# Differential attention: head squares as one instruction per four heads, sums on VectorE

## The reference, cut to what matters

```python
sc = einsum('bqhcd,bshcd->bhcqs', qb, k) * scale
p = softmax(sc, axis=-1)
a = p[:, :, 0] - lam * p[:, :, 1]
o = einsum('bhqs,bshe->bqhe', a, v)
o = rmsnorm(o, subln_g) * (1.0 - lam_init)   # over the 128 columns of a head
return o.reshape(b, s, nh * 2 * dh) @ w_out
```

## Time and profile before

| what | value |
|---|---|
| median of three launches | 1442.16 us (1442.08 to 1443.78) |
| profiled execution | 1442.12 us, its span 1440.3 us |
| TensorE busy | 1422.6 us, 99% of the span |
| VectorE busy | 858.5 us, 60% |
| ScalarE busy | 747.9 us, 52% |
| granted TensorE clock | 1.00 of full speed |
| differential attention's tasks | about 267 to 307 us of the span |

### The profile page before, as it was taken

One profiled execution on the slowest core, in us unless ns is written; L12 is line 12 of the kernel. 1 busy time (PEld: TensorE's weight loads), 2 busy tenths in 40 slices (PEclk: granted clock), 3 DMA queues, 4 the chain that ended last, 5 costly groups with the idle time before them and its releaser, 6 DMA issues.

```text
span 1440.3 us, 20791 instructions
## 1 busy us (share of the span) xinstructions
PE 1422.6 (99%) x6864; PEld 1184.1 (82%) x6864; DVE 858.5 (60%) x1113; ACT 747.9 (52%) x1216; POOL 90.9 (6%) x115
## 2 busy tenths in 40 slices
PE   9999999999999999999999999999999999999999
PEld 7888888778888888888888988888888898888887
DVE  5555575767555565555655665555657756565654
ACT  6444464656444454444546654444545465465553
POOL 2110110012111000000100000000013000000000
PEclk9999999999999999999999999999999999999999
DMA  9877746315655656556463155566565513555551
GB/s 304 245 224 219 219 155 210 118 59 160 190 189 189 203 162 190 189 187 195 157 219 111 37 160 189 188 187 201 181 208 161 176 60 104 178 167 181 184 183 53
DMA packets 189938, 248.21 MB, mean 172 GB/s; under 512 B 15194, under 2 KB 128101, under 8 KB 189760
## 3 DMA queue, kind: packets, MB, share of 16 engines
q1 hardware_dynamic: 187904, 241.35, 53.1%
q0 software_dynamic: 1984, 6.21, 1.9%
HBM read 246.33 MB, written 1.17 MB: 172 GB/s over the span
## 4 chain that ended last, share of the span: by engine, by line
PE 93%; DVE 3%; ACT 1%; issue 1%; POOL 1%; DMA 0%; SPq 0%; ACTq 0%; DVEq 0%; POOLq 0%
PE ps L272 26%; PE ps L274 26%; PE ps L273 26%; PE ps L760 2%; PE ps L796 2%; PE ps L555 1%; PE ps L785 1%; PE ps L285 1%; DVE h L476 1%; PE ps L367 1%; PE ps L962 1%; PE ps L286 1%; PE ps L290 1%; PE ps L332 1%; PE ps L331 1%
## 5 line engine op out<-in xcount | busy, mean ns | idle before, releaser
L265 DVE TENSOR_TENSOR wlo<-raw,whi 128x1024 fp32r<-128x1024 f32 x450 | 549.5, 1230 | 393.4 <-ACT whi L257 393.2
L257 ACT CAST whi<-raw 128x1024 fp32r<-128x1024 f32 x450 | 469.9, 1051 | 361.5 <-PE ps L274 344.9
L272 PE MATMUL ps<-whi,xhi 128*128 128x512 f32 x1280 | 499.9, 391 | 0.0
L274 PE MATMUL ps<-whi,xlo 128*128 128x512 f32 x1280 | 498.2, 389 | 0.0
L273 PE MATMUL ps<-wlo,xhi 128*128 128x512 f32 x1280 | 498.0, 389 | 0.0
L274 PEld LDWEIGHTS ps<-whi,xlo 128*128 128x128 f32 x1280 | 240.2, 188 | 50.3
L272 PEld LDWEIGHTS ps<-whi,xhi 128*128 128x128 f32 x1280 | 240.3, 188 | 49.5
L273 PEld LDWEIGHTS ps<-wlo,xhi 128*128 128x128 f32 x1280 | 240.3, 188 | 49.3
L272 PE MATMUL ps<-whi,thi 128*128 128x512 f32 x400 | 160.5, 401 | 0.0
L274 PE MATMUL ps<-whi,tlo 128*128 128x512 f32 x400 | 156.4, 391 | 0.0
L273 PE MATMUL ps<-wlo,thi 128*128 128x512 f32 x400 | 156.0, 390 | 0.0
(11 more groups left out here) (181 smaller groups left out, 1141.2 us busy)
## 6 DMA issues: line engine op xcount, KB each, us to landing
raw<-in_ffn_wg_dram SPq DMA_DIRECT2D x176, 256.0 KB, 2.9
raw<-in_ffn_wu_dram SPq DMA_DIRECT2D x176, 256.0 KB, 3.1
raw<-in_ffn_wd_dram SPq DMA_DIRECT2D x176, 256.0 KB, 3.0
raw<-in_w_ffn_up_dram SPq DMA_DIRECT2D x88, 256.0 KB, 3.5
raw<-in_w_in_dram SPq DMA_DIRECT2D x80, 256.0 KB, 3.3
raw<-in_diff_w_in_dram SPq DMA_DIRECT2D x48, 256.0 KB, 3.0
raw<-in_na_w_in_dram SPq DMA_DIRECT2D x48, 256.0 KB, 3.1
raw<-in_w_ffn_down_dram SPq DMA_DIRECT2D x44, 256.0 KB, 3.0
```

The costliest lines, as they stand in the source:

```text
L257: nc.scalar.copy(whi[:, s], raw[:, s]).then_inc(s_hi, 1)
L265: nc.vector.tensor_tensor(wlo[:, s], raw[:, s], whi[:, s].bitcast(F32), ALU.subtract).then_inc(s_lo, 1)
L272: nc.tensor.matmul(outs[t], ahi[:, c], whi[:, s, i], start=start, stop=False)
L274: last = nc.tensor.matmul(outs[t], alo[:, c], whi[:, s, i], start=False, stop=stop)
```

## The change

`squares(g)` becomes one ScalarE instruction over the 512 elements of a PSUM bank, without accumulator, in place of four over 128 elements with one accumulator each. VectorE gets a reduction over four groups of 128 elements, from the buffer of squares `sqa` into `sso`, between the wait for the squares and the product that stood there. Because VectorE now reads the buffer, ScalarE waits before groups 2 and 3 for the sums of two groups earlier (`s_ss`) and no longer for its own squares (`s_sq`).

```diff
@@ -814,12 +814,8 @@
                 act.wait_ge(s_pv, b + 4 * (g + 1))
                 if g >= 2:
-                    act.wait_ge(s_sq, g - 1)
-                for hd in range(4):
-                    ins = nc.scalar.activation(sqa[:, (g % 2) * 512 + hd * P:(g % 2) * 512 + (hd + 1) * P],
-                                               ps[:, Y + g, hd * P:(hd + 1) * P], ACT.Square,
-                                               accum_out=sso[:, g // 2, 4 * (g % 2) + hd:4 * (g % 2) + hd + 1])
-                ins.then_inc(s_sq, 1)
+                    act.wait_ge(s_ss, g - 1)
+                nc.scalar.activation(sqa[:, (g % 2) * 512:(g % 2 + 1) * 512], ps[:, Y + g], ACT.Square).then_inc(s_sq, 1)
@@ -860,6 +856,8 @@
                 steps.done(nc.vector.tensor_tensor(ri[:, t, inv2], ri[:, t, c], ri[:, t, c], ALU.mult))
                 dve.wait_ge(s_sq, g + 1)
+                steps.done(nc.vector.tensor_reduce(sso[:, t, c], sqa[:, (g % 2) * 512:(g % 2 + 1) * 512].rearrange(
+                    "p (g c) -> p g c", g=4), AX_X, ALU.add))
                 nc.vector.tensor_tensor(sso[:, t, c], sso[:, t, c], ri[:, t, inv2], ALU.mult).then_inc(s_ss, 1)
```

## The result

The changed kernel takes 1446.26 us (median of 13 executions, 1444.45 to 1448.01) against 1442.24 us before (median of 13, 1441.89 to 1443.78). The ratio over all executions is 1.0025 with a 95% interval of 1.0016 to 1.0033: slower by about a quarter of a per cent. Between the medians lie 4.0 us. The forecast was 2.4 us and 1444.5, and the measured median lies 0.06 us above the upper end of its range, 1446.2. The executions don't lie around their median but in three clumps: three at 1444.45 to 1444.61, seven at 1445.96 to 1446.36, three at 1447.37 to 1448.01. The first clump is where the forecast put the time; what sets the second apart is the subject of most experiments.

The account below looks back on a forecast made before the run. VectorE was taken to bound the attention's second half and the chain to the last transposes; delays of 0.51 + 0.52 + 0.66 + 0.70 = 2.39 us for groups 0 to 3 gave 1444.5 us, 8-in-10 range 1443.1 to 1446.2.

Parts of the forecast that it names:

- VectorE sets the pace of this stage: Second half of the attention's tasks, 284 to 300 us: VectorE, busy 14.96 of 16 us, is the limit, not TensorE.
- ScalarE's saving is worth nothing: One square per group saves ScalarE about 0.48 us, but VectorE comes later anyway, so nothing is gained on the path.
- the room that the prediction had counted: Slack before VectorE's later instructions in groups 0, 1 and 2, 0.41 us together, already counted as given back.
- The waits cost nothing: ScalarE's new wait for sums of two groups earlier, before groups 2 and 3, finds them ready and costs nothing.
- the delay is carried to the end whole: Behind the last transposes at 306.40 us nothing absorbs the 2.39 us, so the program ends that much later.
- rival 1: TensorE's pause before the last transposes grows to 2.7 us and its clock falls, costing 3.1 us: 1447.6 us, chance 0.07.
- one of the prediction's own signs of being wrong: Matmuls behind the last transposes, after 308.8 us, starting more than 0.23 us apart would show the forecast wrong.
- The price of a fall: A slow TensorE stretch of 6.2 us, as at the program's start, would lose half of it, 3.1 us.
- The other 0.75: Chance of no distinguishable change, below about 0.2% or 2.9 us; it holds most of the forecast and the absorbed delay.
- the dear reduction: VectorE's reduction costs 1.21 us, as for 1024 elements, because of SBUF reading or its groups: 1446.7 us, chance 0.06.
- the absorbed delay: The delay is made up later in the program and the time stays at 1442.2 us; chance 0.06.
- ScalarE's exponentials were the limit: ScalarE's late exponentials limit the tasks and hide the reductions; at most 0.41 us gained, 1441.7 us, chance 0.04.

Follow-up runs that it names:

- e4: Changed kernel with the four accumulating squares kept on ScalarE beside VectorE's reductions: median 1446.10 us, quick group 1444.6.
- e5: Changed kernel without the reductions, one ScalarE square per group, product reading each head's first column: 1441.88 us, ratio 0.9997 to the kernel before.
- e6: Kernel before with 1, 2 or 3 unused VectorE reductions in front of group 3's product: medians 1444.48, 1445.10 and 1445.88 us.
- e1: Changed kernel with eight warming products on TensorE in the pause before the last four transposes: 1444.50 us, ratio 1.0018 to the kernel before.
- e2: Kernel before with the change for head groups 2 and 3 only: median 1445.40 us, quick group 1443.9.
- e3: Kernel before with the change for head groups 0 and 1 only: median 1443.54 us, quick group 1443.5.

## Why the prediction was right and where it was not

- **VectorE sets the pace of this stage:** right. Four reductions, 0.69 us each (0.67 taken), moved the chain by 2.44 us (2.39 forecast), each group within 0.05 us.
- **ScalarE's saving is worth nothing:** right beside the reductions, shown by e4 (same time without it). Without them it is worth 0.4 us (quick groups of e5), as much as the room that the prediction had counted.
- **The waits cost nothing, and the delay is carried to the end whole:** right; behind 313.75 us the matmuls are as dense as before, and the changed kernel's quick executions lie at 1444.5 us, the forecast.
- **The clock:** the step that failed is the chance given to rival 1. The prediction worked out the pause of 2.7 us (2.73 measured), said that the trace had none of this length to test it, and then gave the fall 7 in 100. It came in most executions: 10 of 13 of the changed kernel are late, and the profiled one shows the low clock right behind the pause. e6 shows that lengthening the pause alone does it, e1 that filling it undoes it. With that, one of the prediction's own signs of being wrong came true: matmuls behind the last transposes start 0.43 us apart, not 0.23. The Trainium skill, "TensorE: Matmul & The Clock Gate", section "HAM oscillation — how this bites in real kernels", names idle gaps as the cause. The runs agree on that. The gaps here are shorter than those of its example, and yet 2.05 and 2.7 us were enough in most executions.
- **The price of a fall:** 3.1 us was half of a slow stretch of 6.2 us, taken from the start of the program. Here the granted clock was low only between 309 and 313 us, and that cost 1.59 us in the trace. Between the first two clumps lie 1.5 to 1.7 us in the six kernels with a long pause. A single such fall gives 1446.1 us, not the 1447.6 of the rival.
- **Chances and range:** slower by over 0.2% had 0.23 and came true at 0.25%, though its interval reaches down to 0.16%. The other 0.75 stood on a smaller change. The upper end of the range was set by the dear reduction and the lower one by the absorbed delay. No part of it was made for a fall of the clock, so that the median came near its upper end is luck. The likeliest case was right in mechanism and short by the clock's term: 2.4 where the medians say 4.0 us.
- **The other rivals** fell: no reduction cost 1.2 us, no delay was absorbed, and ScalarE's exponentials were the limit only for the few tenths that the prediction had given back.

What stays open: why late executions occur once in six also in the kernel before, of which only e5's place was seen; what decides whether a pause of a given length is followed by a fall; and whether the third clump (1447.4 to 1448.0) is a second fall in one execution. Its size suggests it, and so does the mean clock: 0.998 or less in 14 of the 16 such executions of the kernels with a long pause, 0.999 or more in all 31 of the second clump. No trace shows it. Open are also the 0.3 us that e2 and e3 have around their spans.

## What to carry to other kernels

When TensorE is 99% busy, look for the short stretches where another engine holds it, and price a change there in full: each microsecond on that chain is one at the end. A delay in front of TensorE has a second price where it lengthens a pause; ask of every pause that grows whether the trace has one as long with a full clock behind it, and if not, give the fall a real chance. Even if it has, one trace is no proof, since the same pause gave both outcomes. Work that must lengthen such a chain belongs into the waits that the chain already has, as the sums of group 3 in GpSimd's 1.41 us.

## What was not expected of the hardware

- Between 1.3 and 2.05 us of pause the share of late executions went from 17 of 101 to 8 of 11, and it grew little up to 2.8 us (8 of 11) and 3.5 us (9 of 10). A pause of one length gives both outcomes in one program, so a single profile can show either.
- Four accumulating squares of 128 columns keep ScalarE for 1.00 us, one of 512 without accumulator for 0.49 us: half of the cost was in the number of instructions and their accumulator reads.
